# A 16-head attention output projection in rounded passes, with the state-space powers moved to another engine

## The reference, cut to what matters

```python
def _mla_output(o_lat, gate, w_uv, w_out):
    v = jnp.einsum('bnhc,chv->bnhv', o_lat, w_uv).reshape(b, n, MLA_WIDTH)
    return (v * jax.nn.silu(gate)) @ w_out          # MLA_WIDTH 2048 -> 1024, for 256 + 512 tokens
...
    lam_bar = jnp.exp(lam_dt)
    b_bar = ((lam_bar - 1.0) / lam)[..., None] * bmat
    powers = jnp.exp(lam_dt[None] * jnp.arange(1, S5_CHUNK + 1)[:, None, None])
```

## Time and profile before

| what | us |
|---|---|
| median of 3 runs | 2124.95 |
| lowest and highest run | 2121.58, 2131.04 |
| span of the profiled execution | 2123.0 |
| PE busy in it | 2008.0 (95%) |
| DVE busy | 1479.0 (70%) |
| ACT busy | 878.7 (41%) |
| POOL busy | 515.9 (24%) |

### The profile page before, as it was taken

One profiled execution on the slowest core, in us unless ns is written; L12 is line 12 of the kernel. 1 busy time (PEld: TensorE's weight loads), 2 busy tenths in 40 slices (PEclk: granted clock), 3 DMA queues, 4 the chain that ended last, 5 costly groups with the idle time before them and its releaser, 6 DMA issues.

```text
span 2123.0 us, 42217 instructions
## 1 busy us (share of the span) xinstructions
PE 2008.0 (95%) x17318; PEld 1577.7 (74%) x17318; DVE 1479.0 (70%) x2087; ACT 878.7 (41%) x1500; POOL 515.9 (24%) x419
## 2 busy tenths in 40 slices
PE   7999998899999999999989979999999999999997
PEld 6787877777885565556555547888877799999885
DVE  3366664468985677666558856888894798898844
ACT  3335543343324444444434036555543544343423
POOL 2553221230017999000001121111111111111000
PEclk9999999999999999999999989999999999999998
DMA  9221443432452122111169724999984423333421
GB/s 370 84 90 60 135 149 122 156 139 77 159 193 67 69 90 85 48 43 43 52 262 369 288 102 131 312 307 306 321 262 169 132 97 111 108 101 107 143 90 40
DMA packets 125711, 317.85 MB, mean 150 GB/s; under 512 B 12128, under 2 KB 58080, under 8 KB 118864
## 3 DMA queue, kind: packets, MB, share of 16 engines
q1 hardware_dynamic: 110240, 243.14, 34.7%
q0 software_dynamic: 10672, 53.14, 6.8%
q10 hardware_dynamic: 4608, 18.88, 2.3%
HBM read 238.69 MB, written 76.41 MB: 148 GB/s over the span
## 4 chain that ended last, share of the span: by engine, by line
PE 82%; DVE 9%; issue 4%; ACT 3%; DMA 1%; POOL 1%; SPq 0%; ACTq 0%; DVEq 0%; POOLq 0%
PE psum L520 15%; PE psum L3587 13%; PE psum L2831 8%; PE psum L1999 7%; PE psum L3011 6%; PE psum L2589 5%; PE psum L2552 3%; PE psum L1192 3%; PE psum L2564 3%; PE psum L2640 2%; PE psum L3181 2%; PE psum L333 2%; PE psum L3240 1%; PE psum L3131 1%; PE psum L2578 1%
## 5 line engine op out<-in xcount | busy, mean ns | idle before, releaser
L2831 PE MATMUL psum<-gate,ring 128*128 128x512 f32 (+1 forms) x512 | 165.4, 486 | 1.2 <-issue 1.2
L3011 PE MATMUL psum<-h,u_w 128*128 128x256 f32 (+1 forms) x768 | 158.8, 353 | 7.9 <-DVE h L2941 5.9
L2831 PEld LDWEIGHTS psum<-gate,ring 128*128 128x128 f32 x512 | 97.2, 190 | 69.3 <-issue 62.7
L520 PE MATMUL psum<-h_split,in_w 128*128 128x512 f32 x600 | 139.0, 391 | 1.5 <-POOL in_w L509 1.5
L3011 PEld LDWEIGHTS psum<-h,u_w 128*128 128x128 f32 x768 | 119.8, 193 | 27.4 <-issue 11.5
L520 PEld LDWEIGHTS psum<-h_split,in_w 128*128 128x128 f32 x600 | 111.9, 188 | 27.2 <-ACT prev L856 2.1
L3544 POOL TENSOR_TENSOR ring<-ring 128x1024 f32<-128x1024 f32 x16 | 54.2, 3385 | 317.9 <-DVE xT L3538 317.9
L509 POOL TENSOR_TENSOR u_w<-ring,u_w 128x512 fp32r<-128x512 f32 x42 | 53.9, 1282 | 275.3 <-ACT u_w L497 231.0
L2681 DVE TENSOR_REDUCE early<-psum 128x1 f32<-128x768 f32 (+1 forms) x96 | 74.8, 780 | 47.5 <-PE psum L2564 45.7
L2589 PE MATMUL psum<-area,ckv_tm 128*128 128x512 f32 (+1 forms) x256 | 102.7, 555 | 1.0 <-ACT area L2715 1.0
L1999 PE MATMUL psum<-x_high,ring_split 128*128 128x512 f32 x272 | 101.1, 393 | 0.0
(11 more groups left out here) (501 smaller groups left out, 5000.4 us busy)
## 6 DMA issues: line engine op xcount, KB each, us to landing
ring<-in_s_glu SPq DMA_DIRECT2D x64, 512.0 KB, 3.5
ring<-in_w_mod SPq DMA_DIRECT2D x48, 512.0 KB, 5.7
c_pow<-made_c_pow SPq DMA_DIRECT2D x32, 576.0 KB, 5.0
ring<-in_s_in SPq DMA_DIRECT2D x32, 512.0 KB, 6.6
made_b_pow<-area POOLq DMA_DIRECT2D x15, 1024.0 KB, 7.1
b_pow<-made_b_pow SPq DMA_DIRECT2D x15, 1024.0 KB, 10.5
ring<-in_w_in SPq DMA_DIRECT2D x25, 512.0 KB, 3.6
made_table<-table_made ACTq DMA_DIRECT2D x16, 768.0 KB, 6.3
```

Of the source, the lines that this page charges most:

```text
L520: ins = nc.tensor.matmul(out, rounded(buffer(u, w)[:, ks]), values(x, k), start=(first and k == 0 and n == 0), stop=(last and k == UNIT_K ...
L2831: ins = nc.tensor.matmul(o, tile_w(("mla_out", 2 * m + k // KD), k % KD), gate2[:, k, a:a + n], start=(k == 0), stop=(k == KE - 1))
L3011: ins = nc.tensor.matmul(o, rounded(u_w[:, u % 4, w, kk * P:(kk + 1) * P]), h3_part(x, k)[:, a:a + size], start=(k == 0 and n == 0), stop= ...
```

## The change

The output projection becomes three rounded passes, as the input projection is. 14 of its 128 steps of k are issued between the waits of the last head. `gate2` is split in a rounded part (ACT, into 16 places that are free at different times) and a rest that DVE writes over `gate2`. Each of the 16 weight slots is rounded by ACT and its rest made by DVE. The tables are made one by one between ACT's roundings, with two buffers in place of four. POOL makes 11 of the b_pow tiles in the heads, DVE keeps four. SP's other transfers move: x comes back into `h2` after POOL's tiles are stored, and the wait for all tables stands ahead of slot `mla_out 15`. The second tile of c_pow and both of b_pow are loaded when the last output tile is done.

```diff
+POOL_B_POW = 11
...
-    s += [("mla_out", i, SLOT, ("mla_out", i)) for i in range(2 * KD)]
+    for i in range(2 * KD):
+        s += [("mla_out", i, SLOT, ("mla_out", i)), (None, i, SLOT, ("mla_out_high", i))]
...
         def angle_load_act(act, m):
-            act.dma_start(table_made[:, m % 4, N_TABLE // 2:N_TABLE], io["angle"][m]).then_inc(angle_loaded[m % 4], 16)
...
+            if m >= 2:
+                act.wait_ge(table_stored[m % 2], 16 * (m // 2))
+            act.dma_start(table_made[:, m % 2, N_TABLE // 2:N_TABLE], io["angle"][m]).then_inc(angle_loaded[m % 2], 16)
+
+        def table_act(act, m):
+
+            if m == 0:
+                angle_load_act(act, 0)
+            if m + 1 < KE:
+                angle_load_act(act, m + 1)
+            cosine, sine = table_made[:, m % 2, 0:N_TABLE // 2], table_made[:, m % 2, N_TABLE // 2:N_TABLE]
+            act.wait_ge(angle_loaded[m % 2], 16 * (m // 2 + 1))
+            nc.scalar.activation(cosine, sine, ACT.Abs).then_inc(act_done, 1)
...
+            act.dma_start(io["table"][m], table_made[:, m % 2, :]).then_inc(table_stored[m % 2], 16)
...
+        def b_pow_early_pool(pool):
+            for m in range(2):
+                pool.dma_start(b_bar_read[m % 2], io["b_bar"][m]).then_inc(b_bar_loaded[m % 2], 16)
+            for m in range(POOL_B_POW):
+                pool.wait_ge(b_bar_loaded[m % 2], 16 * (m // 2 + 1))
+                if m >= 2:
+                    pool.wait_ge(b_pow_stored[m % 2], 16 * (m // 2))
+                for o, a, b, op in b_pow_parts(m, b_pow_made[m % 2], b_bar_read[m % 2], pool_tmp):
+                    nc.gpsimd.tensor_tensor(o, a, b, op).then_inc(pool_done, 1)
+                    pool.wait_ge(pool_done, pool_count.up("s5", "b_pow", m))
+                pool.dma_start(io["b_pow"][m], b_pow_made[m % 2]).then_inc(b_pow_stored[m % 2], 16)
...
             if h == HEADS:
                 turn(UNITS * h - 2)
+                mla_out_steps_pe(pe, 0, 3, 6)
                 turn(UNITS * h - 1)
+                mla_out_steps_pe(pe, 0, 6, 9)
                 values(h - 1)
+                mla_out_steps_pe(pe, 0, 9, 11)
                 up_values(h - 1)
+                mla_out_steps_pe(pe, 0, 11, 14)
...
             turn(n + 3)
             project(h + 1, "rope")
+            if h == HEADS - 1:
+                mla_out_steps_pe(pe, 0, 0, 3)
...
+        def mla_out_steps_pe(pe, m, k0, k1):
+
+            for k in range(k0, k1):
+                i, kk = 2 * m + k // KD, k % KD
+                if kk == 0:
+                    pe.wait_ge(*at("mla_out_w", "rest", i))
...
+                for w, x in ((0, 0), (0, 1), (1, 0)):
+                    weights = rounded(slot_split(("mla_out" if w else "mla_out_high", i))[:, kk * P:(kk + 1) * P])
+                    for a in (0, HALF):
+                        values = gate2_low[:, k, a:a + HALF] if x else gate2_high[k][:, a:a + HALF]
+                        ins = nc.tensor.matmul(mla_out_part(m, a, a + HALF), weights, rounded(values),
+                                               start=(k == 0 and w == 0 and x == 0), stop=(k == KE - 1 and w == 1))
...
+        def mla_out_act(act):
+            gate2_high_act(act, KE - 1)
+            made = 0
+            for i in range(2 * KD):
+                mla_out_w_act(act, i + 2)
+                while made < min(KE, 4 * (i + 1) // 3):
+                    table_act(act, made)
+                    made += 1
...
         def mla_out_dve(dve):
             v = nc.vector
+            for k in range(KE - 2, KE):
+                gate2_low_dve(dve, k)
             h3_gain_dve(dve)
-            dve.wait_ge(x_back, 2 * 16)
             for m in range(KD):
-                b_pow_dve(dve, 2 * m)
-                if m < KD - 1:
-                    b_pow_dve(dve, 2 * m + 1)
+                mla_out_w_dve(dve, 2 * m + 2)
+                if m < B_POW_BESIDE:
+                    b_pow_dve(dve, POOL_B_POW + m)
+                if m == 0:
+                    dve.wait_ge(x_back, 2 * 16)
+                v.tensor_scalar(h2[:, m, :], h2[:, m, :], ALPHA_2, None, ALU.mult).then_inc(dve_done, 1)
+                dve.wait_ge(dve_done, dve_count.up())
+                mla_out_w_dve(dve, 2 * m + 3)
                 dve.wait_ge(*at("mla_out", m))
...
                 if n == slot_of[("head", HEADS - 1)] + RING:
-                    sp.wait_ge(*at("scores", UNITS * HEADS - 1))
-                    sp.wait_ge(c_late_stored, 16 * (KE - LATE_C_POW))
-                    sp.dma_start(xT[:, :, :], io["x_kept"]).then_inc(x_back, 16)
-                    sp.dma_start(ctxT[:, :, :], io["ctxT"]).then_inc(x_back, 16)
-                if n == slot_of[("mla_out", 12)]:
+                    sp.wait_ge(*at("s5", "b_pow", POOL_B_POW - 1))
+                    for i in range(2):
+                        sp.wait_ge(b_pow_stored[i], 16 * ((POOL_B_POW + 1 - i) // 2))
+                    sp.dma_start(h2[:, :, CTX:TC], io["x_kept"]).then_inc(x_back, 16)
+                    sp.dma_start(h2[:, :, 0:CTX], io["ctxT"]).then_inc(x_back, 16)
+                if n == slot_of[("mla_out", 15)]:
                     for who in ("pe", "act", "dve", "pool"):
                         sp.wait_ge(*at("end", "heads", who))
                     for made in table_stored:
-                        sp.wait_ge(made, 16 * KE // 4)
+                        sp.wait_ge(made, 16 * KE // 2)
                     for tile in range(2):
                         b_bar_sync(sp, tile)
-                        for h in range(2):
-                            c_pow_sync(sp, tile, h)
-                if n == slot_of[("mla_out", 13)]:
+                    for h in range(2):
+                        c_pow_sync(sp, 0, h)
+                if n == slot_of[("s5_in", 2)]:
+                    sp.wait_ge(*at("mla_out", KD - 1))
+                    for h in range(2):
+                        c_pow_sync(sp, 1, h)
                     for tile in range(2):
                         sp.wait_ge(b_pow_stored[tile], 16)
                         b_pow_sync(sp, tile)
```

More of the change, by code:

```diff
@@ L1874, in build @@
         b_bar_out = h2_flat[:, 5632:5632 + 2 * N_B]
+        b_pow_made = [h2_flat[:, i * N_B_POW:(i + 1) * N_B_POW] for i in range(2)]
+        b_bar_read = [h2_flat[:, 5120 + i * N_B:5120 + (i + 1) * N_B] for i in range(2)]
         sq3, rms = q_abs, q_raw
@@ L2299, in b_pow_pool @@
                     pool.dma_start(b_bar_in[m % 2], io["b_bar"][m + 2]).then_inc(b_bar_loaded[m % 2], 16)
-                if m % 2 == 1 and 5 <= m:
-                    ln2.add_pool(pool, (m - 1) // 2 - 1)
-            ln2.add_pool(pool, KD - 2)
+                if m >= POOL_B_POW + 2:
+                    ln2.add_pool(pool, m - POOL_B_POW - 1)
+            for k in range(KE - 1 - POOL_B_POW - 1, KD - 1):
+                ln2.add_pool(pool, k)
             ln2.pair_pool(pool)
@@ L2799, in head_dve @@
             if h == HEADS:
+                for k in range(10, KE - 2):
+                    gate2_low_dve(dve, k)
                 gated(h - 1)
@@ L2814, in head_dve @@
                     c_pow_steps_dve(dve, late + 1, late + 3)
+                if pair == 1 and h == HEADS - 1:
+                    for k in range(1, 5):
+                        gate2_low_dve(dve, k)
+                if pair == 2 and h == HEADS - 1:
+                    gate2_low_dve(dve, 5)
                 normalize_dve(dve, n + 2 * pair + 1)
@@ new lines, in mla_out_at, with mla_out_part, gate2_high_act @@
+        def mla_out_at(m):
+            return (((m + 1) % 2) * 2 + 1) * BANK - HALF
+        def mla_out_part(m, a, b):
+            return flat(mla_out_at(m) + a, mla_out_at(m) + b)
+        def gate2_high_act(act, k):
+            act.wait_ge(*at("gated", k))
+            if k == 0:
+                act.wait_ge(*at("kr_copied"))
+            if k == 1:
+                act.wait_ge(*at("s5", "c_pow", KE - 1))
+            if k == 3:
+                act.wait_ge(*at("q_pos", HEADS - 1))
+            if k == 4:
+                act.wait_ge(*at("scores", UNITS * (HEADS - 1) - 1))
+            if k == 7:
+                act.wait_ge(c_late_stored, 16 * (KE - LATE_C_POW))
+            if k == 10:
+                act.wait_ge(*at("scores", UNITS * HEADS - 1))
+            if k == 14:
+                act.wait_ge(*at("up_values", HEADS - 1))
+                act.wait_ge(*at("turned", UNITS * HEADS - 1))
+            nc.scalar.activation(rounded(gate2_high[k]), gate2[:, k, :], ACT.Copy).then_inc(act_done, 1)
+            act_count.up("gate2", "high", k)
@@ new lines, in gate2_low_dve, with mla_out_w_act @@
+        def gate2_low_dve(dve, k):
+            dve.wait_ge(*at("gate2", "high", k))
+            nc.vector.tensor_tensor(rounded(gate2_low[:, k, :]), gate2[:, k, :], gate2_high[k], ALU.subtract).then_inc(dve_done, 1)
+            dve_count.up("gate2", "low", k)
+        def mla_out_w_act(act, i):
+            if i >= 2 * KD:
+                return
+            need_slot(act, ("mla_out", i))
```

(10 more changed lines are left out.)

179 lines of the change are left out of this document (102 added, 77 removed).

## The result

| | before | after |
|---|---|---|
| median of 20 runs each, us | 2125.44 | 2136.35 |
| lowest and highest | 2118.16, 2132.63 | 2128.27, 2148.87 |
| span of the profiled execution | 2123.0 | 2126.5 |

The changed kernel is slower, by 0.5%: ratio 1.0052, 95% interval 1.0038 to 1.0066. The forecast was 2110, 0.7% faster, with a range of 2094 to 2132. The profiled execution of after took 2128.27, the fastest of its 20, so its trace shows less of the loss than the median does.

What follows compares the result with a forecast made beforehand. PE, 82% of the chain, bounds the kernel; in the shortened output projection ACT's tables take over. Terms -15.9 - 0.8 + 0.7 + 1 = -15 took the span from 2123.0 to 2108, median 2110; range 2094 to 2132.

Steps and rivals of the forecast that it cites:

- What it does to DVE in the heads: Heads beside POOL's new products: each 0.1 us longer, 0.7 us in all, the slower DVE being hidden by PE.
- Rival (d): Heads: DVE's products each wait 0.9 us, two a head on PE's path, 12 us, total 2122; chance 0.05.
- POOL's time: b_pow tiles in the heads: 16.2 us a tile, eleven of them 178 us, done at 1038.
- ACT's chain: Output projection: ACT's tables, each waiting for a store's landing, become the bound at 7.3 us a table.
- L: Landing time of a table store in the output projection, taken as 4.1 us; a table costs L + 3.2.
- rival (b): Output projection: stores land at the median 6.3 us, 9.5 a table, ACT's wait replaces the matmuls, 2145; chance 0.16.
- last head: 14 output steps, 14.7 us, fit between its waits while PE ends only 4.8 us later than 1080.4.
- moved transfers: c_pow of tile 1, two b_pow tiles and three slots, 5 MB, start at the stage's end: 1 us more.
- PE's price: Output projection: 1.047 us a step of three passes, 128 steps 134.0 us against 165.4.
- Rival (e): Last head: the early start of 14 steps is worth nothing, hidden behind ACT's tables; no separate chance, already in the forecast.
- (c): POOL's b_pow tiles late, done at 1104 in place of 1083 at the phase end, total 2131; chance 0.05.
- (a): Output projection: table stores land as the first did, 3.3 us, 6.5 a table, total 2097; chance 0.18.

Runs made afterwards that it cites:

- run without products: Changed kernel with POOL's 66 two-input products left out, each store's buffer filled once with zeros instead: median 2103.85 us, ratio 0.9924 to the kernel before.
- three buffers: Changed kernel with a third buffer for ACT's tables, the angle load of m + 1 waiting for store m - 2; output not right: ratio 0.997 to before.
- load behind: Changed kernel with ACT's load of angle m + 1 issued behind the store of table m, two buffers as before: ratio 1.01 to the kernel before.
- before plus products: Kernel before with the same 66 POOL products added after its tables, on scratch values, without loads or stores: ratio 1.0154 to the kernel before.
- angles apart: Changed kernel with angles loaded into two rooms of their own, so no load waits for a store, two table buffers: ratio 0.9969 to before.

## Why the prediction was wrong

**The step that failed** is "What it does to DVE in the heads": 0.7 us in all, and 26.8 came. It read the period of two pairs of heads, 26.70 with POOL at work and 26.60 without, and carried the 0.1 over to POOL's new work. But an unchanged period says only that DVE's idle time was not used up. Four heads of the kernel before show how much of it was. Stretches 726 to 833 (POOL at its tables) and 860 to 967 (POOL idle):

```profile
726.00:833.00 107.00, 103.34 (x506) 63.93 (x504) 83.40 (x132) 47.12 (x92) 99.36 (x75) 1.00 0.25 89
860.00:967.00 107.00, 104.21 (x508) 64.35 (x507) 68.68 (x133) 47.12 (x92) 0.00 (x0) 1.00 0.12 41
```

POOL at its tables already cost DVE 14.7 us in four heads, 3.7 a head, all within DVE's idle time. There 41 us of POOL's 99 went to instructions with a single operand (16 of 2.5 to 2.7 us), and those with two took 0.6 to 1.8 us. The products are two-operand throughout and take 2.27 us:

```profile
L2326 POOL TENSOR_TENSOR early<-early,power 128x1024 f32<-128x1024 f32 x44 | 99.7, 2266 | 4.6 <-DMA early<-made_b_bar 1.9
```

DVE's busy time per head is 17.1 us alone, 20.8 beside the tables and 27.9 beside the products (143.42 of 160 at 31.1 a head), in a period of 26.6. That sum would have shown that the cover was gone. It would not have given the price: 27.9 - 26.6 is 1.3 us a head, and 4.5 came. DVE is still idle for 10% of the stretch; the rest of the loss is that longer instructions of DVE stand one behind the other on the path from PE over ACT and DVE back to PE. A part of it is PE's own: its 881 matmuls of the seven heads take 187.2 us and not 180.9, with a granted clock of 0.98 and not 1.00 in the mean, in the stretch in which PE waits for DVE.

**Rival (d)** had mechanism and place, and the prediction's own sign for it, heads over 26.9 us apart, is the one that showed; its price was wrong twofold. It gave DVE 0.9 us a product and two on PE's path, 12 us. The c_pow products that met one of POOL's lose 1.95 each, the scalings 0.6 to 1.7, and more than two a head are on the path. Its chance of 0.05 rested on the same 0.1 us a head, and the forecast's sign hung on it. The rule of the **Trainium skill** on SBUF interfaces shared with VectorE (GPSIMD Engine Reference, Key points) was cited as agreeing and then set aside because PE covers it; the runs agree with the rule for the products, and setting it aside was the error. The prediction told only half of it: the page names DVE instructions in a 2-port mode too. The scalings read one tensor and were slowed; that they ran in such a mode no trace shows.

**POOL's time** was right: 16.2 us a tile forecast and 15.9 measured, the last store issued at 1033.6, 1038 forecast. Of the reading of the 3.385 us row as a wait for DVE nothing was tested by itself.

**ACT's chain** was right in kind. Its size came out near, 7.3 us a table forecast and (1228.4 - 1116.4) / 15 = 7.47 measured, partly by luck: L was 4.8 in the mean and not 4.1, close to the 5.0 at which rival (b) begins, while the work beside it was 2.98 and not 3.2, and the last table waited for no landing. The price for L that the prediction took from the **Trainium skill** (DMA: Bandwidth & Descriptors, Anatomy of one DMA), 3.8 us, stands there for transfers that GpSimd issues; for these stores of ACT the traces show 3.24 to 3.26 for five of the 14 and a mean of 4.8. The **last head** was right: values begun 4.3 us later than before by my numbers (1072.5 against 1068.2), 4.0 in the traces. From there to PE's end of the stage I had 157.3 us, and 152.7 came (1251.2 - 1098.6; before 177.6). The 4.6 are made of: first store 17.9 us behind the start of the values and not 21.5, -3.6; fifteen tables at 0.17 more, +2.5; 22.8 behind the last store and not 26.3, -3.5, of which 2.0 were put in for a fallen clock and did not come (the last eight steps took 8.73, forecast 8.4 + 2.3). The moved transfers were to cost 1 us; the stretch behind the last residual is 1.2 shorter. The run without products is the forecast without its failed term: 2103.85, where I had 2110.

**PE's price** of 1.047 us a step measured 1.057. **Rival (e)** held, (c) appeared where POOL's tile grew from 15.9 to 20.9 us, and neither (a) nor (b) did.

**What is left open.** The loss in the heads is not a constant: with the same head code the traces show 26.5 to 26.9 four times, 30.7 with three buffers and 33.1 with the load behind. The granted clock goes some way with it: over the seven heads it is 0.98 or 0.99 in the four, 0.96 with three buffers, 0.97 with the load behind and 0.95 in before plus products, which lost 32.5. Which is cause and which effect is not shown. That may be why after's 20 runs spread over 20.6 us and before's over 14.5, and why its median lies 8 above the profiled run, but there is one trace of each kernel. How the loss divides between longer instructions on the path and the slower PE was not separated. Whether products cut finer or coarser would do as well was not tried, nor whether DVE's c_pow products, the largest item on the chain, would do less harm elsewhere. Of the two ways to free the tables, the one to take is the angles apart.

## What to carry to other kernels

When work is moved to an idle POOL, sum what it adds to DVE's busy time in that stretch and hold the total against the period of the loop; an earlier stretch where POOL cost nothing says only that the slack was not used up. If the total comes near the period, the loss can be several times the excess (here 4.5 us a head for 1.3), so follow the path as well. Cut POOL's two-operand instructions short: here four pieces took the loss from 26.8 to 1.5 us, for 5.0 us more of POOL's time a tile. Before counting a stage's gain on PE, name the chain that will bound it next and give it room: a buffer reused as soon as its store lands puts the store's landing into every round, and a load issued behind the store in the same queue does the same.

## What the hardware showed

A DVE instruction on two SBUF operands went from 1.36 to 3.31 us in the mean beside POOL instructions of 2.27 and to 1.71 beside pieces of 0.78: what it lost, 1.95 and 0.35, is near the length of one of POOL's in the first case and half of one in the second. One trace, that of after, shows the step. These are products of the same size; the first begins in POOL's pause between two tiles, the last 2.18 us before the end of a POOL instruction (start us, us, what):

```profile
889.76 1.36 DVE L2209 TENSOR_TENSOR ctxT<-q_pos,power 128x1152 f32<-128x1152 f32 x1
...
895.05 2.55 POOL L2326 TENSOR_TENSOR early<-early 128x1024 f32<-128x1024 f32 x1
895.42 3.39 DVE L2209 TENSOR_TENSOR xT<-q_pos,power 128x1152 f32<-128x1152 f32 x1
```

The last lost 2.03 us. Another, at 961.52, began 1.77 us before the end of POOL's and lost 1.63 (2.99 in all). Between 860 and 1026 nine of these products began while one of POOL's ran, and each lost what was left of it, less 0.15 us: in this trace the two took turns by whole instructions. The five that began in a pause took 1.36 us.

Instructions that read PSUM lost nothing (958 ns). POOL's fills, which read nothing, left the two-operand product at 1358 ns but took the one-operand scaling from 621 to 1366 ns. I had expected them to leave both alone.
